# Head loop with combined vector forms, shorter root chains, one norm chain, and the last gate's modulation moved to the output projection

## The reference

```
mod = silu(c) @ ada_w + ada_b                # per group: sh1, sc1, g1, sh2, sc2, g2
h   = rmsnorm(x) * (1 + sc1) + sh1
P   = h @ w_in                               # 8 retention heads, 8 differential heads
o   = concat(retention(P), diff_attention(P)) @ w_out
x   = x + g1 * rmsnorm(o)
h   = rmsnorm(x) * (1 + sc2) + sh2
x   = x + g2 * rmsnorm(PEER(h))              # routing over 128 x 128 experts
```

## Time and profile before

| | us |
|---|---|
| median of 3 runs | 3749.97 (3749.48 to 3754.81) |
| the profiled execution's own time | 3747.88 |
| its span, first to last instruction | 3745.9 |
| TensorE busy in the span | 3389.8 |
| VectorE busy in the span | 2743.4 |
| GpSimd busy in the span | 1059.3 |

### The profile page before, as it was taken

How to read it: one execution, slowest core, us unless ns; L and a number is a source line. 1 busy time by engine, 2 the same in 40 slices (tenths; PEclk the granted TensorE clock), 3 DMA queues, 4 the chain that set the end, 5 groups by cost and what they waited for, 6 DMA issues and landing times.

```text
span 3745.9 us, 48877 instructions
## 1 busy us (share of the span) xinstructions
PE 3389.8 (90%) x19267; PEld 3067.4 (82%) x19267; DVE 2743.4 (73%) x4155; ACT 975.3 (26%) x1137; POOL 1059.3 (28%) x532
## 2 busy tenths in 40 slices
PE   7798888888759689989799999999999999999996
PEld 1387767777759644688799999999999999999996
DVE  1378888888940346889588787788767787787877
ACT  1122222222121210134223322332233223323331
POOL 0043223233224107730132232232212332232320
PEclk9798999999979789999899999999999999999998
DMA  7454444444332332034689888888878988988985
GB/s 318 184 181 147 148 151 148 162 151 151 127 149 90 157 135 79 34 130 200 242 332 346 335 331 337 331 333 332 333 263 319 332 330 330 339 327 319 349 335 208
DMA packets 197192, 893.93 MB, mean 239 GB/s; under 512 B 81621, under 2 KB 82414, under 8 KB 108686
## 3 DMA queue, kind: packets, MB, share of 16 engines
q1 hardware_dynamic: 150926, 555.73, 40.4%
q0 software_dynamic: 46080, 335.56, 23.0%
HBM read 854.38 MB, written 35.77 MB: 238 GB/s over the span
## 4 chain that ended last, share of the span: by engine, by line
PE 62%; issue 20%; DVE 8%; POOL 7%; DMA 2%; ACT 0%; SPq 0%; POOLq 0%; DVEq 0%; ACTq 0%
PE ps_all L835 15%; PE ps_all L889 9%; PE ps_all L895 9%; PE ps_all L890 9%; PE ps_all L842 8%; POOL sb_w_low L1717 6%; PE ps_all L805 6%; DVE sb_hot L1601 2%; PE ps_all L627 2%; PE ps_all L629 2%; PE ps_all L628 2%; DVE sb_hot L1597 1%; DMA sb_g_ring<-table_scratch 1%; DVE sb_mix_lo L1482 0%; DVE sb_raw_lo L1541 0%
## 5 line engine op out<-in xcount | busy, mean ns | idle before, releaser
L1131 ACT ACTIVATE sb_raw_hi<-sb_raw_ring 128x2048 fp32r<-128x2048 f32 x256 | 490.7, 1917 | 1232.4 <-DMA sb_raw_ring<-in_v_t 515.2
L889 PE MATMUL ps_all<-sb_w_hi,sb_raw_hi 128*128 128x352 f32 x2048 | 658.7, 325 | 26.4 <-DVE sb_w_lo L1620 20.7
L835 PE MATMUL ps_all<-sb_h_hi,sb_raw_hi 128*128 128x352 f32 x2048 | 662.3, 326 | 5.3 <-issue 5.3
L835 PE MATMUL ps_all<-sb_h_lo,sb_raw_hi 128*128 128x352 f32 x2048 | 661.1, 324 | 5.1 <-issue 5.1
L890 PE MATMUL ps_all<-sb_w_lo,sb_raw_hi 128*128 128x352 f32 x2048 | 657.2, 322 | 0.0
L1541 DVE TENSOR_TENSOR sb_raw_lo<-sb_raw_ring,sb_raw_hi 128x2048 fp32r<-128x2048 f32 x256 | 585.3, 2287 | 86.1 <-ACT sb_raw_hi L1131 86.1
L1760 POOL DMA_INDIRECT sb_gather_ring<-in_u_tab,sb_kept x160 | 261.5, 1634 | 845.5 <-DVE sb_kept L1640 666.2
L1717 POOL TENSOR_TENSOR sb_w_low<-sb_w_raw,sb_w_high 128x2048 fp32r<-128x2048 f32 (+1 forms) x64 | 267.1, 4174 | 738.3 <-ACT sb_w_high L965 738.3
L1760 POOL DMA_INDIRECT sb_gather_ring<-in_v_tab,sb_kept x160 | 272.8, 1705 | 681.7 <-DVE sb_acc_a L1652 484.0
L889 PEld LDWEIGHTS ps_all<-sb_w_hi,sb_raw_hi 128*128 128x128 f32 x2048 | 386.7, 189 | 27.5 <-issue 27.2
L835 PEld LDWEIGHTS ps_all<-sb_h_lo,sb_raw_hi 128*128 128x128 f32 x2048 | 387.8, 189 | 6.0 <-issue 6.0
(11 more groups left out here) (237 smaller groups left out, 5317.5 us busy)
## 6 DMA issues: line engine op xcount, KB each, us to landing
sb_raw_ring<-in_u_t SPq DMA_DIRECT2D x128, 1024.0 KB
sb_raw_ring<-in_v_t SPq DMA_DIRECT2D x128, 1024.0 KB
sb_arena<-in_ada_wt SPq DMA_DIRECT2D x128, 512.0 KB, 5.8
sb_arena<-in_ada_w SPq DMA_DIRECT2D x8, 4096.0 KB
sb_w_raw<-in_w_t SPq DMA_DIRECT2D x32, 1024.0 KB, 5.4
sb_w_raw<-in_w_v SPq DMA_DIRECT2D x32, 768.0 KB, 4.2
sb_g_ring<-table_scratch SPq DMA_DIRECT2D x64, 352.0 KB
table_scratch<-sb_stage SPq DMA_DIRECT2D x7, 2816.0 KB, 8.2
```

Source lines behind the costliest of these rows:

```text
L835: last = mm(acc, raw_hi[:, r[0], kk * P:(kk + 1) * P], part[:, kk, :], start=i == 0, stop=False)
L889: mm(accs[c], v, w_hi[:, slots[e], :], start=e == 0, stop=False)
L1131: acti(raw_hi[:, k % 2, :], raw_ring[:, k % RAW, :], ACT.Copy).then_inc(S["un_hi"], 1)
```

## The change

Four things are changed together.

- **Pieces.** Parts 3 to 5 of the modulation (48 columns a group) stay in the head loop, 12 pieces a head and not 16. The last part, gate2, is computed on VectorE between the odd-block copies of the output projection: 32 pieces, 8 in each of four rounds, through a ring of two places (`col_ring_w`), against a copy of silu(c) loaded again into `silu_w`. Its loads stand in SyncE's queue between the `wo_load`s; `coef_products(1)` and post1's load move behind them. A transpose in bank 4, an addition and two stores for it stand in the routing, at head 1.
- **Norm.** `ret_norm` takes both groups at once; `rsqrt` has three refinements everywhere.
- **Forms.** ALiBi is now given in the scaled unit and `dif_soft` multiplies and adds in one instruction, so the scaling of `nmax` falls away. Some tensor_tensor and tensor_scalar instructions are written as scalar_tensor_tensor.
- **Release by tile.** Piece 7 raises `proj_v` after each token tile; `evacuate` of tiles 4 to 7 waits for its own tile. TensorE waits for its own last matmul of piece 7 and then raises `proj`. VectorE's order of pieces changes: 0, 1; 2, 3; 4 to 6; 7, 8; 9; 10, 11.

```diff
-LATE = (MODS - 2) * KD
+LATE = 3 * KD
+HEAD_COLS = LATE // 8
-PIECES = 2 * LATE // 8
+PIECES = 2 * HEAD_COLS
+LAST_PIECES = 2 * KD
...
             sp.wait_ge(S["out_te"], 2 * HEADS)
-            sp.dma_start(post1_sb, post1.partition_broadcast(P)).then_inc(S["coef_in"], 16)
+            for g in range(GROUPS):
+                sp.dma_start(silu_w[g], silu_d[g:g + 1, :].partition_broadcast(P)).then_inc(S["silu_w"], 16)
+            def last_col_load(n):
+                wait(sp, "col_used", HEADS * PIECES + n - 1)
+                sp.dma_start(col_ring_w[:, n % 2, :], ada_wt[LATE + n // 2, :, n % 2, :]).then_inc(S[f"col_in{n % 2}"], 16)
+            for n in range(2):
+                last_col_load(n)
...
-            with sp.Fori(1, D // WOC) as b:
-                for half in range(2):
-                    wo_load(b, half)
+            for n in range(2, 2 * (D // WOC)):
+                wo_load(n // 2, n % 2)
+                for c in range(2 * n - 2, 2 * n if n < 2 * (D // WOC) - 1 else LAST_PIECES):
+                    last_col_load(c)
+            sp.wait_ge(S["col_used"], HEADS * PIECES + LAST_PIECES)
+            sp.dma_start(post1_sb, post1.partition_broadcast(P)).then_inc(S["coef_in"], 16)
...
+                if n == 9:
+                    sp.wait_ge(S["gate2_row"], 1)
+                    for g in range(GROUPS):
+                        sp.dma_start(mod_d[g, 5 * D:MODS * D].rearrange("(c p) -> c p", p=P), gate2_rows[g * KD:(g + 1) * KD, :])\
+                            .then_inc(S["gate2_out"], 16)
...
-                last.then_inc(S["proj"], 1)
+                        if n == 7:
+                            last.then_inc(S["proj_v"], 1)
+                if n < 7:
+                    last.then_inc(S["proj"], 1)
+                else:
+                    wait(pe, "proj_v", NT * h + NT)
+                    pe.sem_inc(S["proj"], 1)
...
-                    wait(pe, "ret_n", 2 * a + u + 1)
+                    wait(pe, "ret_n", a + 1)
...
-                wait(act, "proj", 8 * h + min(n + 1, 4) if n < 4 else 8 * h + 8)
+                if n < 4:
+                    wait(act, "proj", 8 * h + n + 1)
+                else:
+                    wait(act, "proj_v", NT * h + n - 3)
...
-                for n in range(4):
+                for n in range(3):
                     link(vec.scalar_tensor_tensor(a, y, -0.5, y, ALU.mult, ALU.mult))
-                    link(vec.tensor_tensor(a, a, v, ALU.mult))
+                    link(vec.scalar_tensor_tensor(a, a, 1.0, v, ALU.mult, ALU.mult))
...
-                vec.tensor_tensor(soft[:, units, m, :], b.rearrange("p (t k) -> p t k", t=TPG), alibi, ALU.add)\
-                    .then_inc(S["dif_sd"], 1)
+                vec.scalar_tensor_tensor(soft[:, units, m, :], b.rearrange("p (t k) -> p t k", t=TPG), DQK ** -0.5, alibi,
+                                         ALU.mult, ALU.add).then_inc(S["dif_sd"], 1)
                 wait(dve, "dif_sd", 4 * a + u + 1)
-                link(vec.tensor_reduce(nmax[:, units, m], soft[:, units, m, :], axis=AX, op=ALU.max, negate=True))
-                vec.tensor_scalar(nmax[:, units, m], nmax[:, units, m], DQK ** -0.5, None, ALU.mult).then_inc(S["dif_m"], 1)
+                vec.tensor_reduce(nmax[:, units, m], soft[:, units, m, :], axis=AX, op=ALU.max, negate=True).then_inc(S["dif_m"], 1)
...
-                link(vec.tensor_scalar(e_g[:, t, :], e_g[:, t, :], 1.0, None, ALU.add))
+                link(vec.scalar_tensor_tensor(e_g[:, t, :], e_g[:, t, :], 1.0, e_g[:, t, :], ALU.add, ALU.max))
...
+            for i in range(D // WOC // 2):
+                for n in range(i * LAST_PIECES // 4, (i + 1) * LAST_PIECES // 4):
+                    half = n % 2
+                    late_piece(n, col_ring_w[:, half, :], [silu_w[g][:, half * PIECE:(half + 1) * PIECE] for g in range(GROUPS)],
+                               half, 16 * (HEADS * PIECES // 4 + n // 2 + 1), HEADS * PIECES + n)
+                for t in range(NT):
+                    wait(dve, "wo_mm", (2 * i + 1) * NT + t + 1)
+                    vec.tensor_copy(o_sb[:, t, (2 * i + 1) * WOC:(2 * i + 2) * WOC], bank(4 + t)[:, 0:WOC]).then_inc(S["wo_dve"], 1)
+            vec.tensor_tensor(gate2_cols, mod_part[:, 0], mod_part[:, 1], ALU.add).then_inc(S["gate2_cols"], 1)
             dve.wait_ge(S["coef_in"], 16 * 5)
             coef_products(1)
```

More of the change, by code:

```diff
@@ L221, in build_program @@
         pair_id = take(2 * SLOTS).rearrange("p (t s) -> p t s", t=2)
+        gate2_bias, gate2_rows = take(P)[0:GROUPS * KD, :], take(P)[0:GROUPS * KD, :]
         at += 6 * ND
@@ L710, in out_transposes @@
                 if w == 0:
-                    wait(pe, "ret_n", 2 * a + 2)
+                    wait(pe, "ret_n", a + 1)
                 else:
@@ L823, in _ @@
                     key_scores(hd - 1)
+                if hd == 1:
+                    pe.wait_ge(S["gate2_cols"], 1)
+                    nc.tensor.transpose(bank(4)[0:GROUPS * KD, 0:P], late_all[:, GROUPS * LATE:SLOTS], ident[:, :])\
+                        .then_inc(S["gate2_t"], 1)
                 query(hd, 1)
@@ L992, in soft_exp @@
                 for m in range(2):
-                    last = acti(soft[:, u, m, :], soft[:, u, m, :], ACT.Exp, scale=DQK ** -0.5, bias=nmax[:, u, m:m + 1],
+                    last = acti(soft[:, u, m, :], soft[:, u, m, :], ACT.Exp, bias=nmax[:, u, m:m + 1],
                                 accum_out=esum[:, u, m:m + 1])
@@ L1423, in late_sums @@
                 dve.sem_inc(S["spare"], 1)
-                link(vec.tensor_tensor(mod_cols[:, :, ds(h * 8, 8)], mod_part[:, 0, :, :], mod_part[:, 1, :, :], ALU.add))
+                link(vec.tensor_tensor(mod_cols[:, :, ds(h * HEAD_COLS, HEAD_COLS)], mod_part[:, 0, :, 0:HEAD_COLS], mod_part[:, 1, :, 0:HEAD_COLS], ALU.add))
             def head_step(h, a, link):
@@ L1441, in head_step @@
                 step(dif_soft, 0, 1)
-                late(0, 1, 2)
+                late(0, 1)
                 step(dif_soft, 2, 3)
-                late(3, 4, 5)
+                late(2, 3)
                 step(dif_combine, 0, 1)
-                late(6)
-                step(ret_norm, 0, 1)
-                late(7, 8, 9)
+                if a is not None:
+                    ret_norm(a, link)
+                late(4, 5, 6)
                 step(dif_combine, 2, 3)
+                late(7, 8)
+                step(dif_norm, 0)
+                late(9)
+                step(dif_norm, 1)
                 late(10, 11)
-                step(dif_norm, 0)
-                late(12, 13)
-                step(dif_norm, 1)
-                late(14, 15)
                 gates_of(0, 1, 2, 3)
@@ L1569, in _ @@
                         .then_inc(S["h2_lo"], 1)
+                if hd == 1:
+                    dve.wait_ge(S["gate2_t"], 1)
+                    dve.wait_ge(S["gate2_bias"], 16 * GROUPS)
+                    vec.tensor_tensor(gate2_rows, bank(4)[0:GROUPS * KD, 0:P], gate2_bias, ALU.add).then_inc(S["gate2_row"], 1)
                 if hd == 5:
```

94 lines of the change are left out of this document (51 added, 43 removed).

## The result

The changed kernel takes 3600.04 us (median of 4 runs, 3598.75 to 3609.93) where the kernel before, on the same chip, takes 3749.72: a ratio of 0.9604 [0.9585, 0.9623], 150 us less. The profiled execution took 3600.15 us, with a span of 3598.2.

The account below looks back on a forecast made before the run. TensorE was taken as the bound, busy for 90% of the span, with head-loop stalls on VectorE. Terms -92 -5.5 -5.6 -4.1 +1.4 +0.3 = -105.5 against the profiled 3747.9 gave 3642 us, range 3590 to 3690.

Parts of the forecast that it names:

- the walk through the turn: Head loop: one turn followed step by step from project(0), ending at 95.7 us, rounded to 96.
- the -92 term: Head loop: 13.2 us less a turn, over seven turns (heads 1 to 7).
- the +1.4 of the release: Head loop, project(7): TensorE's wait for its own last matmul, 0.2 us in each of seven turns.
- my two branches: Head-loop turn: first, combines 2, 3 meet GpSimd's pass, 95.7 us; second, combines precede it, next differential norm stalls, 96.4.
- Head 0 and the last step: Head 0: edge stall and slow restart go, -5.5 us; step after the last head: shorter serial VectorE chain, -5.6.
- Refinements elsewhere: Residual and last tiles: three links of 0.2 us saved in seven chains on the path, -4.1 us.
- (A): Head loop: TensorE becomes the bound, combines arrive in time, turns of 87 to 89 us, 3580 to 3594; chance 12%.
- (B): Head loop: the locks move along, most stalls stay, turns of 102 us, 3683; chance 17%.
- (C): Output projection: moved pieces delay it or its tail by 10 to 35 us, 3652 to 3677; chance 12%.
- (D): Output projection: the two-place ring gives no overlap, 10.1 us a piece, slower at 3783; chance 3%.
- (E): Whole kernel: the change does nothing, since stalls only moved, 3745 to 3752 us; chance 1%.
- The theory Load: Head loop, from the experiments: the turn follows VectorE's work, each part gives its own share and the shares add up.

Follow-up runs that it names:

- the filled slot: The changed kernel with one piece of VectorE moved into its idle time ahead of the second softmax pair: 3582.70 us, ratio 0.9555.
- a pure move: The changed kernel with one piece moved from behind combines 2, 3 to ahead of them, no work added: 3635.18 us, ratio 0.9700.

## Why the prediction was right, and where it was off

**Bound and mechanism: right.** TensorE's stalls on VectorE were the reserve, and they were what went. The turn without stalls was put at 86.6; with the filled slot it is 87.58 - 0.3 - 0.25 = 87.0.

**VectorE's load: right.** 80 forecast, 79.1 to 80.5 measured. The 6.1 us stall on the retention norm is gone.

**The step that failed is the walk through the turn**, in the words "Should the combines slip in ahead of the pass, the next differential norm meets the next pass instead and stalls dif_values for about as long; I reach 96.4 on that branch too". It mis-sized the -92 term: with the +1.4 of the release it makes -90.6, and that stretch measured -129.3. The combines did slip in ahead. The norm then met its pass too, but only with its last instruction, which is not held. There is a third way between my two branches, 89.8 to 91.2 us long, and the kernel takes it. The branches themselves are real: undone refinements give 95.66 on the second (96.4 forecast), two chains, the old softmax start or a piece moved give 95.3 to 95.4 on the first (95.7 forecast). That the kernel escapes the second by 0.1 to 0.2 us was not foreseen and is luck, and the result is inside the range by 10 us only. Of the forecast's signs, the norm without a stall, the gates and the output projection came; turns of 96, a stall on the combines and a clock of 0.96 (0.98 to 1.00 measured) did not, and a stall on a differential norm came, without one on the combines beside it.

Two sizes put the walk 2.4 us late. After project(3)'s pass it had VectorE at 59.8; measured, from 431.04, it is 57.4 (488.44). It had the retention norm end at 49, measured 46.6 (477.68): I charged the pass under it in full, but it holds only the link at 471.62, for 1.66 of its 3.49 us. The statistics at the head of the norm read PSUM, and the earlier trace rows with L1355 had shown that such instructions run on. Eight passes of 32.8 us hold VectorE for 22.4 in that turn, added up from the rows that are longer than their fellows.

**Stall and restart.** The forecast has 6.5 of stall, 1.9 of restart and 0.7 for the gates in a turn, 9.1; the kernel has 2.17, 1.4 in every second turn and none, 2.9, and 0.3 for `proj`. From 86.6 that gives 89.8, against 90.5 measured. 0.7 stays unexplained; 0.4 of it is there in the order without stalls too.

**Forms: wrong in the softmax.** I took -0.3 to -0.8 a turn for the scalings of nmax, and said that the pass would block the next piece instead. It does (459.90), but the second half of the softmax pair gets done first, and undoing it costs 4.8 us a turn by the first branch. The price lies in the place, not in the instruction. The other rewritten forms were taken as 0 and were not undone by themselves; in the rows a gate's addition takes 0.28 us against 0.22 before, a link 0.16 in both forms, and both forms are held.

**Release by tile: right as a stall, its worth less than thought.** The own wait is 0.30 a turn (0.2 taken). The gates' stall is 0 instead of 0.7. Alone on the kernel before it gives nothing, because VectorE came late to its gates there.

**Head 0 and the last step.** -6.3 for -5.5. The last step is 9.9 shorter for 5.6: VectorE begins ret_decay 2.8 us behind TensorE's scores (887.68 against 884.88), 6.3 behind them before (1026.76 against 1020.47). Those 3.5 were not in the sum. Undone one by one, the release gives back 4.2 of this step, one chain 2.8 and the refinements 2.7 (55.1, 53.7 and 53.6 us against 50.9), together 9.7; but runs that leave all three as they are have 51.3 to 53.5 there, so the single values are rough. Of head 0's 6.3, the release undone gives back 2.3.

**Refinements elsewhere.** -3.2 at the residual, but +1.2 to the end, where four chains should have given -2.4 and the gate2 row costs 0.3. With four refinements again the two stretches are 64.4 (+0.9) and 2412.5 (-0.1), so the runs show neither that the -3.2 comes from the refinements nor that the last four chains lie on the path: both stay open.

**The moved pieces: right.** The last one ends at 1113.2, 177 us into the stage (176 forecast). The copies of one block came late (1072.31, three in a row without a wait) and TensorE did not wait for them.

**The rivals.** (A) had the mechanism nearly right, 87 to 89 for 90.5. (B), (C), (D) and (E) did not happen. The order with the filled slot, 3582.70, is the turn of (A). The theory Load fell with a pure move: 36 us for no work.

## What to carry over

When one engine's instructions are held for whole passes of another, a turn's length jumps: list the few results that the bounding engine waits for, and read how far each starts from the next pass. A margin of 0.1 us was worth 5 us a turn here, so a walk with an error of 2 us should count every branch within 2 us, and the range should span them. What a part is worth depends on the others: one chain gave 21 us alone and cost 41 when undone. Here the best step was to fill an idle slot of the helping engine, since that moves all later results at once.

## What the runs showed of the hardware

- A VectorE instruction with an input in PSUM (L1397, L1436, bn_stats), and a tensor_reduce from SBUF, run at full speed under GpSimd's two-input pass. So do a reciprocal from SBUF (128 elements, 952 to 956 ns in all 32 of L1442 of the changed kernel, passes falling on it at 615.19 and 796.11) and a tensor_scalar of one element (0.21 us in the better order at 390.60, under the pass of 390.29). Links and scalings of two elements and more and the reductions of the pieces are held to its end, and take up to 5.5 us. The trace agrees with the Trainium skill, "SBUF — State Buffer", section "SBUF: two separate sides", on instructions with two SBUF inputs. The one-input scaling held for 4.11 us is a tensor_scalar, which the same section names among the operations that can contend with GpSimd, and the trace agrees there too.
- The holding goes both ways: in the head loops of these runs a pass of 1536 columns takes 3.4 to 4.5 us, one of 2048 4.5 to 5.6, the longer ones where a reduction of VectorE was running as it began (3.86 us at 491.38, with 0.5 us of one left; 3.45 at 501.18).
- The same stall of 2.17 us is followed by a slow restart in one turn and not in the next. Behind 501.76 the 384-wide matmuls start 0.32 us apart, behind 592.91 they start 0.17 apart. The windows (last columns: granted clock, DMA share, GB/s) give the two levels, near 1.2 and at 2.4 GHz:

```profile
502.60:506.20 3.60, 3.60 (x15) 3.60 (x14) 3.57 (x3) 0.62 (x4) 2.03 (x1) 0.53 0.21 46
593.70:597.30 3.60, 3.60 (x24) 3.60 (x23) 3.56 (x3) 0.67 (x4) 2.11 (x1) 1.00 0.20 39
```

That is the alternation of 91.2 and 89.8. What differs between the two turns the traces do not show.
